# Hybrid diffusion step: the last expert's weight pieces held behind a scatter and the final tiles' loads

## The reference

```
xg = h[idx]                                        # 80 rows for each expert
y  = (silu(xg @ w_e1) * (xg @ w_e3)) @ w_e2 * gate
x  = x + gate2 * scatter_add(y)                    # over 16 experts
out = x * rsqrt(mean(x*x) + 1e-6) * g_final        # y_prompt, y_sample
```

## Time and profile before

| | |
|---|---|
| median of 3 runs | 3310.93 us (3310.5 to 3312.26) |
| profiled execution | 3311.59 us, its span 3309.4 us |
| TensorE busy | 3238.3 us, 98% |
| VectorE busy | 2121.0 us, 64% |
| ScalarE busy | 1391.4 us, 42% |
| granted TensorE clock, mean | 0.991 |
| DMA | 787.25 MB, mean 238 GB/s |

### The profile page before, as it was taken

One profiled execution on the slowest core, in us unless ns is written; L12 is line 12 of the kernel. 1 busy time (PEld: TensorE's weight loads), 2 busy tenths in 40 slices (PEclk: granted clock), 3 DMA queues, 4 the chain that ended last, 5 costly groups with the idle time before them and its releaser, 6 DMA issues. The chain is left out here.

```text
span 3309.4 us, 39728 instructions
## 1 busy us (share of the span) xinstructions
PE 3238.3 (98%) x15947; PEld 2508.5 (76%) x15947; DVE 2121.0 (64%) x1875; ACT 1391.4 (42%) x1271; POOL 356.9 (11%) x445
## 2 busy tenths in 40 slices
PE   7999999999999999999999999979999999999997
PEld 4788888888888999998888888746666666666664
DVE  4355555565552777773233243279999999999997
ACT  3221222221111455452121222257777777777775
POOL 0020010020000000001111112100111111111102
PEclk9999999999999999999999999989999999999999
DMA  9575554485553111125354455379999999999999
GB/s 395 213 234 176 205 178 175 159 266 193 189 181 129 41 47 35 40 105 204 126 174 140 153 169 190 132 256 382 386 393 399 390 385 388 392 395 388 387 393 337
DMA packets 143918, 787.25 MB, mean 238 GB/s; under 512 B 19888, under 2 KB 30672, under 8 KB 63936
## 3 DMA queue, kind: packets, MB, share of 16 engines
q1 hardware_dynamic: 101344, 666.40, 52.2%
q0 software_dynamic: 42448, 119.03, 12.1%
HBM read 718.11 MB, written 67.25 MB: 237 GB/s over the span
## 5 line engine op out<-in xcount | busy, mean ns | idle before, releaser
L102 DVE TENSOR_TENSOR w_lo<-w_stage,w_hi 128x2048 fp32r<-128x2048 f32 x379 | 863.5, 2287 | 93.0 <-ACT w_hi L97 91.7
L97 ACT ACTIVATE w_hi<-w_stage 128x2048 fp32r<-128x2048 f32 x379 | 727.3, 1920 | 294.7 <-PE e_ps L109 294.7
L107 PE MATMUL ps<-w_hi,hT_hi 128*128 128x512 f32 (+1 forms) x1440 | 563.6, 391 | 0.0
L109 PE MATMUL ps<-w_hi,hT_lo 128*128 128x512 f32 (+1 forms) x1440 | 555.0, 385 | 0.0
L108 PE MATMUL ps<-w_lo,hT_hi 128*128 128x512 f32 (+1 forms) x1440 | 554.9, 385 | 0.0
L107 PE MATMUL e_ps<-w_hi,xgT_hi 128*80 128x512 f32 x1020 | 401.7, 394 | 0.0
L108 PE MATMUL e_ps<-w_lo,xgT_hi 128*80 128x512 f32 x1020 | 400.8, 393 | 0.0
L109 PE MATMUL e_ps<-w_hi,xgT_lo 128*80 128x512 f32 x1020 | 398.2, 390 | 0.0
L601 DVE TENSOR_TENSOR w_lo<-w_raw,w_hi 128x2048 fp32r<-128x2048 f32 (+1 forms) x72 | 161.8, 2247 | 345.7 <-ACT w_hi L460 345.7
L107 PE MATMUL ps<-w_hi,xT_hi 128*128 128x512 f32 x960 | 377.9, 394 | 0.0
L109 PE MATMUL ps<-w_hi,xT_lo 128*128 128x512 f32 x960 | 374.2, 390 | 0.0
(11 more groups left out here) (371 smaller groups left out, 4502.7 us busy)
## 6 DMA issues: line engine op xcount, KB each, us to landing
w_stage<-in_w_e SPq DMA_DIRECT2D x384, 1024.0 KB, 8.1
w_stage<-in_w_ada SPq DMA_DIRECT2D x96, 1024.0 KB, 6.9
w_raw<-in_w_in SPq DMA_DIRECT2D x64, 1024.0 KB, 5.0
w_stage<-in_w_o_gm SPq DMA_DIRECT2D x16, 1024.0 KB, 8.0
w_stage<-in_w_o_mla SPq DMA_DIRECT2D x16, 1024.0 KB, 5.1
w_stage<-in_w_out SPq DMA_DIRECT2D x16, 1024.0 KB, 5.0
acts<-evacuated POOLq DMA_DIRECT2D x60, 256.0 KB, 4.2
side<-acts POOLq DMA_DIRECT2D x40, 256.0 KB, 5.4
```

The source lines that it names most:

```text
L97: act.activation(dst, src, ACT.Copy).then_inc(st.hi, 1)
L102: dve.tensor_tensor(dst, src, hi.bitcast(F32), ALU.subtract).then_inc(st.split, 1)
L107: pe.matmul(out, x_hi, w_hi, start=first, stop=False)
L109: return pe.matmul(out, x_lo, w_hi, start=False, stop=last)
```

## The change

Eight loads of `w_e2` of expert 15 (pieces 24 to 31) are issued by SyncE in the same order, but before piece 26 it waits for a semaphore that GpSimd raises when it has issued the scatter of expert 14, before piece 28 for one that GpSimd raises after the gather and the loads of tiles 0 to 2, and before piece 30 for the same one after tile 3's load. Tiles 0, 1, 3 and 4 are loaded with one DMA of whole rows, tile 2 still with two. The gather takes its indices from `rows` directly, without the index copy; the gate copy comes after the loads of tiles 0 to 2. The variance is no longer formed on VectorE from both sums: one operation makes a bias of the first half's sum (`f_shift`), and the root takes the second half's sum, scaled, with that bias. VectorE's order becomes: tiles 0, 1, 2, `out(LAST, 0)`, `l_add(0)`, tiles 3, 4, `out(LAST, 1)`, `l_add(1)`, the last rows.

```diff
-            last(LAST, n0 + 3 * PB, 0)
+            for q in range(PB):
+                if q == 2:
+                    sp.wait_ge(scatter_begun, 1)
+                if q == 4:
+                    sp.wait_ge(f_begun, 1)
+                if q == 6:
+                    sp.wait_ge(f_begun, 2)
+                load(n0 + 3 * PB + q, q, E2[LAST, q // (PB // 2), q % (PB // 2)])
...
+                if isinstance(e, int) and e == LAST - 1:
+                    pool.sem_inc(scatter_begun, 1)
                 pool_wait(pool, scattered, 16 * e + 16, y_free)
...
             def load_x(t):
-                for h in range(2):
-                    pool.dma_start(f_x[t % N_F][h][:], M.xn[bass.ts(t, P), bass.ts(h, D // 2)]).then_inc(f_in[t % N_F], 16)
-
-            pool.tensor_copy(cur_s[:], rows[:, LAST:LAST + 1]).then_inc(idx_s, 1)
-            pool.tensor_copy(cur_gate[:], gates[:, LAST:LAST + 1]).then_inc(idx_s, 1)
-            pool_wait(pool, idx_s, 2 * LAST + 2, passed)
+                if len(f_x[t]) > 2:
+                    pool.dma_start(f_x[t][2], M.xn[bass.ts(t, P), :]).then_inc(f_in[t], 16)
+                else:
+                    for h in range(2):
+                        pool.dma_start(f_x[t][h], M.xn[bass.ts(t, P), bass.ts(h, D // 2)]).then_inc(f_in[t], 16)
+
             pool_wait(pool, x_tr, 3 * LAST + 6, passed)
             pool.indirect_dma_start(out=xg[:, 0:D], out_offset=None, in_=M.xn,
-                                    in_offset=bass.IndirectOffsetOnAxis(ap=cur_s[:, 0:1], axis=0)).then_inc(gathered, 16)
-            for t in range(TT):
-                if t == 3:
-                    pool_wait(pool, s.used, NW + NP * (LAST - 1) + N0 + 3 * PB, passed)
-                if t == 4:
-                    pool_wait(pool, h_tr, LAST + 2, passed)
+                                    in_offset=bass.IndirectOffsetOnAxis(ap=rows[:, LAST:LAST + 1], axis=0)).then_inc(gathered, 16)
+            for t in range(3):
                 load_x(t)
+            pool.sem_inc(f_begun, 1)
+            pool.tensor_copy(cur_gate[:], gates[:, LAST:LAST + 1]).then_inc(idx_s, 2)
+            pool_wait(pool, s.used, NW + NP * (LAST - 1) + N0 + 3 * PB, passed)
+            load_x(3)
+            pool.sem_inc(f_begun, 1)
+            pool_wait(pool, h_tr, LAST + 2, passed)
+            load_x(4)
...
             def f_root(t):
-                act.wait_ge(f_var, t + 1)
-                act.activation(fst[:, 3, t:t + 1], fst[:, 2, t:t + 1], ACT.Sqrt).then_inc(f_std, 1)
+                act.wait_ge(f_sq, 2 * t + 2)
+                act.wait_ge(f_bias, t + 1)
+                act.activation(fst[:, 3, t:t + 1], fst[:, 1, t:t + 1], ACT.Sqrt, bias=fst[:, 2, t:t + 1], scale=1.0 / D).then_inc(f_std, 1)
...
-            def f_variance(t):
-                dve.wait_ge(f_sq, 2 * t + 2)
-                dve.tensor_tensor(fst[:, 2, t:t + 1], fst[:, 0, t:t + 1], fst[:, 1, t:t + 1], ALU.add).then_inc(f_sum, 1)
-                dve.wait_ge(f_sum, t + 1)
-                dve.tensor_scalar(fst[:, 2, t:t + 1], fst[:, 2, t:t + 1], 1.0 / D, EPS, ALU.mult, ALU.add).then_inc(f_var, 1)
+            def f_shift(t):
+                dve.wait_ge(f_sq, 2 * t + 1)
+                dve.tensor_scalar(fst[:, 2, t:t + 1], fst[:, 0, t:t + 1], 1.0 / D, EPS, ALU.mult, ALU.add).then_inc(f_bias, 1)
...
                 for h in range(2):
-                    x = f_x[t % N_F][h][:]
+                    x = f_x[t][h]
                     dve.scalar_tensor_tensor(x, x, fst[:, 4, t:t + 1], g_final[:, bass.ts(h, D // 2)], ALU.mult, ALU.mult).then_inc(f_ok, 1)
+                    if h == 0 and t < 2:
+                        f_shift(t + 1)
...
-            out(LAST, 0, n0 + 3 * PB + 4)
-            f_variance(0)
-            l_add(0)
+            f_shift(0)
             for t in range(TT):
-                if t == TT - 1:
-                    out(LAST, 1, n0 + 4 * PB)
-                    l_add(1)
+                if t == 3:
+                    out(LAST, 0, n0 + 3 * PB + 4)
+                    l_add(0)
+                if t >= 3:
+                    f_shift(t)
                 f_normal(t)
-                if t + 1 < TT:
-                    f_variance(t + 1)
-            dve.wait_ge(l_sq, 2)
-            dve.tensor_tensor(rst[:, 2:3], rst[:, 0:1], rst[:, 1:2], ALU.add).then_inc(l_sum, 1)
-            dve.wait_ge(l_sum, 1)
-            dve.tensor_scalar(rst[:, 2:3], rst[:, 2:3], 1.0 / D, EPS, ALU.mult, ALU.add).then_inc(l_var, 1)
+            out(LAST, 1, n0 + 4 * PB)
+            l_add(1)
+            dve.wait_ge(l_sq, 1)
+            dve.tensor_scalar(rst[:, 2:3], rst[:, 0:1], 1.0 / D, EPS, ALU.mult, ALU.add).then_inc(l_bias, 1)
```

More of the change, by code:

```diff
@@ L2062, in phase_experts @@
     g_final = Map(nc, M.phase_at + 2 * X_END + X_END // 4 * 3 + 6144).new("g_final_rows", [P, D], F32)
[L2063 to L2067, removed]
+    f_at = (X_END, 2 * X_END + X_END // 4 + 4 * D, None, 4 * (D + 16), 4 * (D + 16) + 2 * 4 * KT * SLOTS)
+    f_x = []
+    for b, at in enumerate(f_at):
+        if at is None:
+            f_x.append([Map(nc, M.phase_at + half).new(f"f_x{b}{h}", [P, D // 2], F32)[:] for h, half in enumerate((2 * X_END + X_END // 4 + 8 * D, X_END + X_END // 4 + 3 * 4 * PIECE))])
+        else:
+            whole = Map(nc, M.phase_at + at).new(f"f_x{b}", [P, D], F32)
+            f_x.append([whole[:, bass.ts(h, D // 2)] for h in range(2)] + [whole[:]])
+    assert 4 * (D + 16) + 4 * D <= 4 * (D + 16) + 2 * 4 * KT * SLOTS and len(f_x) == TT
     LAST = EXPERTS - 1
@@ L2084, in phase_experts @@
         shift_in, x_sc, inv_out, issued = sem("r_shift_in"), sem("e_x_scaled"), M.pool_sem("r_inv_out"), sem("r_issued")
[L2085 to L2088, removed]
+        f_in, f_out, g_in = [M.pool_sem(f"f_in{b}") for b in range(TT)], [M.pool_sem(f"f_out{b}") for b in range(TT)], sem("f_g_in")
+        scatter_begun, f_begun = sem("scatter_begun"), sem("f_begun")
+        f_sq, f_bias, f_std, f_inv, f_ok, rows_y_ok, last_out = (
+            *(sem(f"f_{n}") for n in ("sq", "bias", "std", "inv", "ok", "rows")), M.pool_sem("last_out"))
+        l_x, l_sq, l_bias, l_std, l_inv, l_ok, l_warm, l_half, l_raw = (sem(f"last_{n}") for n in ("x", "sq", "bias", "std", "inv", "ok", "warm", "half", "raw"))
         clear_finished(nc, M)
@@ L2186, in load_x @@
             def load_x(t):
-                for h in range(2):
-                    pool.dma_start(f_x[t % N_F][h][:], M.xn[bass.ts(t, P), bass.ts(h, D // 2)]).then_inc(f_in[t % N_F], 16)
-            pool.tensor_copy(cur_s[:], rows[:, LAST:LAST + 1]).then_inc(idx_s, 1)
-            pool.tensor_copy(cur_gate[:], gates[:, LAST:LAST + 1]).then_inc(idx_s, 1)
-            pool_wait(pool, idx_s, 2 * LAST + 2, passed)
+                if len(f_x[t]) > 2:
+                    pool.dma_start(f_x[t][2], M.xn[bass.ts(t, P), :]).then_inc(f_in[t], 16)
+                else:
+                    for h in range(2):
+                        pool.dma_start(f_x[t][h], M.xn[bass.ts(t, P), bass.ts(h, D // 2)]).then_inc(f_in[t], 16)
             pool_wait(pool, x_tr, 3 * LAST + 6, passed)
             pool.indirect_dma_start(out=xg[:, 0:D], out_offset=None, in_=M.xn,
-                                    in_offset=bass.IndirectOffsetOnAxis(ap=cur_s[:, 0:1], axis=0)).then_inc(gathered, 16)
-            for t in range(TT):
-                if t == 3:
-                    pool_wait(pool, s.used, NW + NP * (LAST - 1) + N0 + 3 * PB, passed)
-                if t == 4:
-                    pool_wait(pool, h_tr, LAST + 2, passed)
-                load_x(t)
+                                    in_offset=bass.IndirectOffsetOnAxis(ap=rows[:, LAST:LAST + 1], axis=0)).then_inc(gathered, 16)
+            for t in range(3):
+                load_x(t)
+            pool.sem_inc(f_begun, 1)
[5 more added lines that the diff above has]
+            load_x(4)
             for t in range(TT):
@@ L2205, in _ @@
                 for h in range(2):
-                    pool.dma_start(dst[:, bass.ts(h, D // 2)], f_x[t][h][:]).then_inc(f_out[t], 16)
+                    pool.dma_start(dst[:, bass.ts(h, D // 2)], f_x[t][h]).then_inc(f_out[t], 16)
             pool.wait_ge(rows_y_ok, 2)
@@ L2291, in f_squares @@
             def f_squares(t):
-                act.wait_ge(f_in[t % N_F], 32 * (t // N_F + 1))
+                act.wait_ge(f_in[t], 16 if len(f_x[t]) > 2 else 32)
                 for h in range(2):
@@ L2297, in f_squares @@
                         act.wait_ge(sil_ok, EXPERTS)
-                    act.activation(pair[0][:], f_x[t % N_F][h][:].rearrange("p (c n) -> p c n", c=2), ACT.Square,
+                    act.activation(pair[0][:], f_x[t][h].rearrange("p (c n) -> p c n", c=2), ACT.Square,
                                    accum_out=fst[:, h, t:t + 1]).then_inc(f_sq, 1)
             def f_root(t):
-                act.wait_ge(f_var, t + 1)
-                act.activation(fst[:, 3, t:t + 1], fst[:, 2, t:t + 1], ACT.Sqrt).then_inc(f_std, 1)
+                act.wait_ge(f_sq, 2 * t + 2)
```

(7 more changed lines are left out.)

## The result

| | before | changed |
|---|---|---|
| median | 3311.01 us (18 runs) | 3316.32 us (3314.42 to 3318.43, 18 runs) |
| ratio of the runs | | 1.0017, 95% interval 1.001 to 1.0023 |
| span of the profiled execution | 3309.4 us | 3314.5 us |
| last 40 matmuls start | 3273.66 | 3273.11 |
| VectorE's last operation ends | 3300.75 | 3305.92 |

The change is slower by 5.3 us. That is inside the stated range of 3307.0 to 3317.0 and in the direction of the small loss in it, but three times that loss (1.8 us), and 0.6 us above the forecast's own narrower range (3311.0 to 3315.7). Part 1 of the profile's page shows the same load: TensorE busy 3237.7 us (before: the earlier trace rows).

A forecast was written before the change was run, and what follows sets the result against it. VectorE's queue bounds the end: tile 2 landing at 3282.0 + 20.5 = 3302.5, 1.8 us later than before, so 3313.4 profiled, median 3312.7; called no change with a small loss (50%), range 3307.0 to 3317.0, own range 3311.0 to 3315.7.

The forecast's parts named there:

- The end is VectorE's queue, and tile 2's landing L becomes critical: At the kernel's end, VectorE's queue and not TensorE sets the end; the new order makes tile 2's landing critical.
- VectorE ends at L + 20.5: VectorE's work behind tile 2's landing: 13.8 us, then 6.7 from `out(LAST, 1)` on; as before if L is 3280.2.
- What is to be won: VectorE's end: `out(LAST, 1)` starting at 3291.0 would end VectorE at 3297.7, a ceiling of 3.0 us gain.
- When tile 2 lands: Tile loads: L = 3280.4 + 3.2 for empty engines - 1.6 for outstanding pieces = 3282.0; bounds 3273 and 3285.
- Turns one for one, halves at half weight: DMA engines: both queues alternate about one for one; tile 2's half loads have turns half as long as a piece's.
- Whole-row loads save nothing: GpSimd's tile loads: four fewer issues of 0.54 us gain nothing, as GpSimd waits for landings anyway; otherwise 2.2 us.
- Index copies gone: 1.6 us earlier gather: GpSimd after the scatter: without the 1.6 us of index copies, the gather follows the landing at once.
- (a): Rival: tiles in time, L at most 3277.2, TensorE sets the end, 3.0 us less, 3307.9; 34%.
- (b): Rival: pieces come too late, TensorE stands still in its last matmuls, VectorE ends 0.9 us later, or about 3314; 9%.
- (c): Rival: halves cost a landing each; merging saves 1.1 us for tile 0 and for tile 1, 3310.5; 4%.
- (d): Rival: the hold does nothing, waits are passed before SyncE reaches them, no order changes, 3310.9; 3%.
- Signs: Trace marks for right: engines empty near 3251 to 3253, scatter landed before 3260, gather issued before 3261, tile 2 after 3280.

The follow-up runs named there:

- e1: Changed kernel with SyncE's three waits taken out, so the last eight pieces are issued as before; 3311.48 us, 1.0001 of before.
- e10: Repetition of e7, pieces 30 and 31 in GpSimd's own queue; 3307.61 us, 0.9993 of before.
- e6: Changed kernel with one SyncE wait only: pieces 30 and 31 held until ScalarE's first square of tile 1; 3308.80 us, 0.9995 of before.
- e3: Changed kernel with the index copy and gate copy back ahead of the last gather; 3316.60 us, 1.0016 of before.
- e2: Kernel before with only SyncE's three waits and GpSimd's two signals added; 3315.54 us, 1.0014 of before.
- e8: Changed kernel, hold included, but with VectorE in the order of the kernel before; 3312.78 us, 1.0005 of before.
- e4: Changed kernel with one SyncE wait only: pieces 30 and 31 held until tile 2 has landed; 3309.64 us, 0.9995 of before.
- e5: Changed kernel with pieces 26 and 27 free, 28 and 29 held for the gather's landing, 30 and 31 for tile 0's; 3312.93 us.
- e7: Changed kernel without SyncE's waits, pieces 30 and 31 issued by GpSimd in its own queue, 31 last; 3307.82 us, 0.999 of before.
- e11: Repetition of e6, pieces 30 and 31 held until ScalarE's first square of tile 1; 3308.14 us, 0.9994 of before.

## Why the prediction was right and wrong

- *The end is VectorE's queue, and tile 2's landing L becomes critical.* Right for this kernel. "VectorE ends at L + 20.5" gives 3305.5 after (measured 3305.92); the rest is the root with a bias, 0.29 us where 0.20 was taken, four times on the path behind tile 2. For e1 it gives 3300.4 (3301.16), but there tile 0 set the end and not tile 2. This second bound, tile 0's landing + 26.25, has no term in the prediction; with tile 0 where it was before, 3275.26, VectorE could not have ended before 3301.5 whatever L was, 0.8 us later than before, so L = 3280.2 was not the break-even.
- *What is to be won.* Nothing contradicts 3.0 us at most; e10 and e6 reach a tail of 24.7 and 24.5 against 27.1 before, 2.4 and 2.6 us.
- *When tile 2 lands.* This term was mis-sized: 3282.0 predicted, 3284.98 measured. It took 3.2 us for a first empty stretch, nothing for a second one, and 1.6 off for pieces outstanding. (a) The first stretch was not there (97% busy from 3251 to 3252), since the hold on pieces 26 and 27 was passed before the scatter was issued. (b) An empty stretch of 4.0 us came later: pieces 26 and 27 had landed by 3255.6, the scatter at 3258.99 (predicted 3258.5), and the gather's issue, predicted to follow at once, started 0.9 us later and ended only at 3262.60, during VectorE's split (e3). (c) "I take a lead of ten turns for the tile queue" was the wrong way round: the signals fired early and the pieces led by 3.5 us, so nothing of them was outstanding when tile 2 landed. Together that is 4.0 us empty and 0.5 more at 87%, where the sum had 1.6; measured from the start of the last matmuls, tile 2 moved by 5.2 us (6.7 to 11.9), and 0.7 of them no run assigns. The upper bound of L, 3285, was formed of the first stretch, which did not occur, and a second of 1.4 us, which was 4.0: that tile 2 landed on it (3284.98), and the time inside the stated range, is partly luck.
- *Turns one for one, halves at half weight.* Right: 286 to 283 packets of 8 KB in the changed kernel, and in e2 555 to 522 packets, but 2.04 to 3.79 MB.
- *Whole-row loads save nothing.* Not shown either way under the hold (e8 against e2: 2.8 us for these, the gather and the statistics). Without the hold it is right: tiles 0, 1 and 2 landed 1.6, 4.1 and 6.7 us after the start of the last matmuls both before and in e1.
- *Index copies gone: 1.6 us earlier gather.* Wrong in the changed kernel: from the scatter's landing to the end of the gather's issue it was 2.7 us before and 3.6 after. The gather starts 0.9 us after the landing, where a copy starts after 0.2, and it fell into a split. In e1, where it did not, 1.9 us remained, 0.8 less than before.
- *Rivals.* (a) was not this kernel; e10 comes near it. (b) did not happen here (17.33 us without a gap), but TensorE stood still in e4, e5, e7 and e11. (c) fell: merging moved no landing in e1. The 2.0 us per load of the Trainium skill ("DMA: Bandwidth & Descriptors", section "Anatomy of one DMA — SWDGE (gpsimd) path") do not add up in a queue either: the whole-row loads of tiles 3 and 4 landed 2.5 us apart in e1 (3282.43, 3284.91), which is the time of their bytes. (d) was half true: the first wait was passed before the scatter was issued, but the second one held.
- *Signs.* Two of the six for "right" failed: the engines were not empty near 3251 to 3253, and the gather had only started before 3261. The scatter's landing before 3260 and those on tile 2 and VectorE were seen.

## What to carry to other kernels

Holding a transfer back helps only if the engines have other work in that stretch, or if it keeps transfers that are not urgent behind one that is. Here the hold left the engines empty for 4 us and then let the pieces run ahead of the gather all the same. Where only the last two pieces were held (e4, e6, e7, e10, e11), the engines stood still or nearly so for at most 2.3 us, and tile 2 landed 1.4 to 4.1 us earlier than before, counted from the start of the last matmuls. To put one transfer behind another use one queue, or the landing of the first, not a signal that the issuing engine raises after it. An order that puts ready work behind loads makes their landings the end of the kernel, that of the first (tile 0, in e1) as well as that of the last.

## What the runs showed of the hardware

- A semaphore raised in GpSimd's program after an indirect DMA lets its waiter go before the DMA is issued: piece 26 left at 3247.07, the scatter's row is 3247.26 to 3252.15. It is the same in e2, e3 and e8, where the piece left 0.18 to 0.19 us before the scatter's row began.
- The gather has its first bytes 0.7 us after its issue when the other queue is silent (e5, and seven more kernels), and 2.8 us (before) to 3.6 us (e8) after it when pieces stream; 3.5 in the changed kernel.
- A GpSimd copy of 80 x 1 takes 0.17 us or lasts until the end of the VectorE split in which it starts (2.02 us in e2, 1.85 in e1). The gather's issue takes 0.93 us, or until 0.8 us after that end (2.69 us in the changed kernel). Direct loads are not affected (0.54 to 0.65 us).
- The two queues get turns by packets and not by bytes: 555 packets of one to 522 of the other carried 2.04 and 3.79 MB (e2).
